# Seven-product down chunks from the first turn in three feed-forwards, from the fourth in the first

## The chip, the cores and the metric

The kernel runs on one core of one Trainium2 chip. The metric is the device time of one execution in microseconds, as the median of several runs. A profile is one execution recorded by the hardware profiler; its span is the time from the first to the last instruction. The engines are TensorE (PE in the rows; PEld is its weight load), VectorE (DVE), ScalarE (ACT), GpSimd (POOL) and the DMA queue of SyncE (SP).

## What is computed

Two decoder layers over 256 tokens of 1024 features, all in fp32. Each layer has a feed-forward, a mixer, a cross-attention to a memory of 256 tokens, and a second feed-forward. There are thus four feed-forwards, f = 0 to 3, and each computes

```python
h = rmsnorm(x, norm_w[layer, i])                      # i = 0 or 3
x = x + 0.5 * ((silu(h @ w_gate) * (h @ w_up)) @ w_down)   # 1024 -> 2816 -> 1024
```

The memory is normed once (`memn = rmsnorm(mem, mem_norm_w)`) and used by both cross-attentions. The rest of the layers is untouched by the change.

## The kernel before

Each fp32 product is made of three passes: both factors are split into a high part (rounded to the fp32r format by ScalarE) and a low part (the rest, by VectorE's subtraction), and TensorE adds high x high, high x low and low x high in PSUM. A split of a weight chunk of 128 x 2048 is one ScalarE copy and one VectorE subtraction.

Weights stream from HBM through a ring of three slots (`raw`, `w_hi`, `w_lo`), one megabyte each. A feed-forward has 11 hidden blocks of 256 features, j = 0 to 10 (`FJ` = 11). Its chunks come in the order gate 0, up 0, gate 1, up 1, down 0, gate 2, up 2, down 1 and so on, 33 in all, counted from `base`: down 0 is chunk `base + 4`. In its turn j TensorE multiplies gate j and up j (16 matmuls of 512 columns and 16 of 256 each) and then down j-1. VectorE and ScalarE in their turn j handle block j: they bring gate and up out of PSUM (banks 0 and 1, banks 2 and 3), scale, take the silu, multiply (`gu`), split the hidden block, and split the chunks that come next. Each engine runs its own list of instructions in the written order and meets the others at semaphores. A turn's order is written out by hand; nothing is planned at run time.

A plain down chunk is a block product with 2 x 2 x 2 = 8 products of 128 x 128 by 128 x 512, that is 24 matmuls (`down`, PSUM banks 4 to 7, which accumulate over all j). A seven-product chunk ("mixed") is one step of a Strassen-Winograd scheme, 7 products or 21 matmuls (`mixed_down`). It needs sums of blocks beforehand: three of the hidden block (`gu_sum`, line 1562), and four of the weights (`w_sum`, line 1556), of which one is written in place into the raw slot; then splits of the seven forms (`forms`, `forms_low`) and of the three weight sums (`Mixed.w_hi`, `Mixed.w_lo`). Products 3, 4 and 5 of the seven accumulate in banks 5, 4 and 7; products 1, 2, 6 and 7 go alone to banks 0, 1, 2 and 3, which TensorE may write only when gate and up of the next block have been read, and ScalarE copies these out (`copied`). The copies are added up in SBUF, in `Mixed.kept`, by accumulating DMAs that POOL issues.

Which chunks are mixed is in `Mixed.TURN` (first mixed j) and `Mixed.COUNT` (how many), one value for each feed-forward:

```python
TURN, COUNT = (4, 1, 1, 1), (5, 8, 8, 8)
```

So down 4 to 8 are mixed in f = 0 and down 1 to 8 in the others; the rest are plain. What TensorE waits for before a mixed chunk stands in its `turn`:

```python
pe.wait_ge(lo_done, j * 3 + (n + 3 - 3))
...
pe.wait_ge(gate_read, j + (f * FJ + 1))
pe.wait_ge(gu_done, j + f * FJ)
used(mixed_down(n + 2, f, j, mixed))
```

The count `lo_done` is brought to that value by VectorE's last step of the mixed turn, `Mixed.w_lo` (line 1618), and `gate_read` by the gate sum (line 1520) of the following turn. Within the chunk TensorE waits for `up_read` (line 1531) before it writes bank 2. SP loads down j+1 into the slot of down j when the latter is split: `lo_done` for a plain chunk, `down_split` for a mixed one.

In f = 0, turn 3 of ScalarE and VectorE also makes the high and low parts of the transposed memory (`mem_hi`, `mem_lo`), and turn 4 of ScalarE takes the squares of the memory's rows. The transposed memory lies in `xn`, where `Mixed.kept` lies too.

Of the kernel before, what the change touches and what calls it, by code (L numbers as in the profile page):

```python
# [20 lines left out]
F32 = mybir.dt.float32  # L21
F32R = mybir.dt.float32r
BF16 = mybir.dt.bfloat16
ALU = mybir.AluOpType
# [6 lines left out]
KT = D // P  # L31
# [5 lines left out]
RING = 3  # L37
# [127 lines left out]
def build(nc, d, out):  # L165
# [3 lines left out]
    with ctx:  # L169
# [277 lines left out]
        class Mixed:  # L447
            TURN, COUNT = (4, 1, 1, 1), (5, 8, 8, 8)
# [201 lines left out]
        def _(sp):  # L650
# [13 lines left out]
            def ffn(layer, which, first=False):  # L664
# [51 lines left out]
                else:  # L716
                    turn(0)
                    turn(1)
# [23 lines left out]
        def _(act):  # L742
# [115 lines left out]
            def ffn(layer, which):  # L858
# [91 lines left out]
                else:  # L950
# [5 lines left out]
                    silu(0)  # L956
                    hi_upto(base + 5)
                    hidden(f * FJ + 1, gu_hi)
                if f == 0:

                    turn(1)
                    turn(2)
                    turn(3, lambda c: mem_hi(range(3 * c, min(3 * c + 3, KT))))
                    turn(4, lambda c: c and squares(1, mem_rows, lambda t, h: act.wait_ge(mem_in, 16), tiles=(c - 1,)),
                         mixed=0)
                else:
                    turn(1, mixed=0)
                first = Mixed.TURN[f]
                turn(first + 1, mixed=1, out=0)
# [389 lines left out]
        def _(dve):  # L1359
# [154 lines left out]
            def ffn(layer, which):  # L1514
# [48 lines left out]

                def mixed_out(i, half, count):
# [23 lines left out]
                def turn_mixed(j, i):  # L1588
# [12 lines left out]
                    gu_sum(i, 0, gu_forms[:, 0:3:2, :], gu_forms[:, 2:5:2, :], gu_forms[:, 1:3, :], ALU.subtract)  # L1601
                    gu_sum(i, 1, gu_forms[:, 5, :], gu_forms[:, 2, :], gu_forms[:, 1, :], ALU.add)
                    gu_sum(i, 2, gu_forms[:, 6, :], gu_forms[:, 3, :], gu_forms[:, 5, :], ALU.subtract)
# [62 lines left out]
                else:  # L1666
                    lo_upto(base + 3)
                    gate_sum(0)
                    lo_upto(base + 4)
                    up_sum(0)  # L1670
                dve.wait_ge(row_read, row_no(norm_no(layer, 3 * which)))
# [7 lines left out]
                else:  # L1679
                    product(0)  # L1680
                    lo_upto(base + 5)
                    hidden_lo(0, gu_hi, gu_lo)
                if f == 0:
                    turn(1)
                    turn(2)
                    turn(3, lambda c: mem_lo(range(3 * c, min(3 * c + 3, KT))))
                first = Mixed.TURN[f]
                turn_mixed(first, 0)
# [587 lines left out]
        def _(pe):  # L2276
# [55 lines left out]
            def down(n, a_hi, a_lo, first, final, last_bank=None, between=lambda i: None, order=BLOCKS,  # L2332
                     second_half=None):

                for i, (t, h) in enumerate(order):
# [12 lines left out]
                    for k in range(2):  # L2348
                        if second_half and i == 0 and k:
# [4 lines left out]
                                        first and k == 0, final and k == 1)  # L2354
# [5 lines left out]
            def mixed_down(n, f, j, i):  # L2360
# [763 lines left out]
```

## Time and profile before

| | |
|---|---|
| Median of 3 runs | 1174.61 us (1174.28 to 1174.80) |
| Profiled execution | 1174.84 us |
| Span of the profiled execution | 1172.7 us |
| TensorE busy | 1165.1 us, 99% |
| VectorE busy | 979.0 us, 83% |
| ScalarE busy | 747.1 us, 64% |
| Mixed down chunks | 29 of 44 |

In the rows a timeline line gives start and duration in microseconds, the engine, the line of the kernel, the operation, output and input tiles, shapes, how many instructions were merged, and in brackets how long the engine had been idle and what ended that. Weight load and matmul overlap, and a matmul's listed duration overlaps the next one's: the spacing of starts is the time that counts.

### The profile page before, as it was taken

The numbers are of one execution on the slowest core, as the hardware profiler recorded it, in microseconds if no ns is written. First come the engines' busy times: TensorE is split into PE (matmuls) and PEld (weight loads), VectorE is DVE, ScalarE is ACT, GpSimd is POOL, SyncE is SP. The second block draws the span as 40 slices with busy tenths as digits, with TensorE's granted clock in tenths as the row PEclk, the third lists the DMA queues.
The fourth block names the chain that finished last, engine by engine and source line by source line (L and its number), as shares of the span: only waits on it lengthen the run. The fifth ranks groups of instructions, "written<-read, shape, count | busy, mean of one in ns | idle before, by whom it ended". The sixth has DMA issues, their size and how long they took to land.

```text
span 1172.7 us, 17754 instructions
## 1 busy us (share of the span) xinstructions
PE 1165.1 (99%) x6754; PEld 1019.4 (87%) x6754; DVE 979.0 (83%) x1134; ACT 747.1 (64%) x960; POOL 141.5 (12%) x139
## 2 busy tenths in 40 slices
PE   9999999999999999999999999999999999999998
PEld 8888889889989888888888888889887898888886
DVE  6689997875657589999988999997886676899997
ACT  7567766854457566777565777564576566677773
POOL 1000021520142010110010011010012121101000
PEclk9999999999999999999999999999999999999999
DMA  9957985454445455899755799846623334669991
GB/s 316 338 193 215 247 255 179 145 181 143 144 144 180 144 181 184 252 264 274 226 196 179 218 261 262 263 144 214 210 90 133 134 119 158 231 206 266 273 260 57
DMA packets 170056, 236.88 MB, mean 202 GB/s; under 512 B 15504, under 2 KB 139792, under 8 KB 169872
## 3 DMA queue, kind: packets, MB, share of 16 engines
q1 hardware_dynamic: 163664, 213.30, 55.5%
q0 software_dynamic: 6192, 22.55, 9.6%
q8 instruction: 38, 0.62, 0.2%
q10 hardware_dynamic: 144, 0.26, 0.1%
q14 instruction: 18, 0.15, 0.0%
HBM read 213.02 MB, written 1.05 MB: 183 GB/s over the span
## 4 chain that ended last, share of the span: by engine, by line
PE 99%; DMA 0%; DVE 0%; POOL 0%; issue 0%; POOLq 0%; ACT 0%; DVEq 0%; SPq 0%; ACTq 0%
PE ps L2302 30%; PE ps L2309 16%; PE ps L2281 15%; PE ps L2282 14%; PE ps L2283 14%; PE ps L2384 1%; PE ps L2569 1%; PE ps L3033 1%; PE ps L2889 1%; PE ps L3056 0%; PE ps L2577 0%; DMA arena<-in_first 0%; PE ps L2994 0%; PE ps L2991 0%; PE ps L2452 0%; PE ps L2641 0%
## 5 line engine op out<-in xcount | busy, mean ns | idle before, releaser
L2302 PE MATMUL ps<-hT,w_parts 128*128 128x512 f32 x1568 | 374.9, 391 | 0.9 <-DVE hT L1416 0.9
L2302 PEld LDWEIGHTS ps<-hT,w_parts 128*128 128x128 f32 x1568 | 290.1, 188 | 59.1 <-DVE w_parts L1443 0.7
L1374 DVE TENSOR_TENSOR w_parts<-raw,w_parts 128x2048 fp32r<-128x2048 f32 x85 | 195.9, 2314 | 57.9 <-ACT w_parts L758 57.8
L758 ACT ACTIVATE w_parts<-raw 128x2048 fp32r<-128x2048 f32 x85 | 162.3, 1920 | 73.5 <-PE ps L2283 71.0
L2309 PEld LDWEIGHTS ps<-hT,w_parts 128*128 128x128 f32 x1568 | 201.4, 191 | 8.0 <-DVE w_parts L1450 0.2
L2309 PE MATMUL ps<-hT,w_parts 128*128 128x256 f32 x1568 | 204.1, 283 | 0.0
L898 ACT ACTIVATE w_parts<-raw 128x2048 fp32r<-128x2048 f32 x79 | 150.9, 1910 | 1.0 <-DMA raw<-in_ffn_w_gate 1.0
L1592 DVE TENSOR_TENSOR w_parts<-raw,w_parts 128x2048 fp32r<-128x2048 f32 x58 | 132.5, 2284 | 0.4 <-ACT w_parts L898 0.4
L2236 POOL DMA_DIRECT2D xn<-arena x42 | 36.5, 868 | 503.7 <-ACT arena L909 503.7
L2281 PE MATMUL ps<-w_parts,hT 128*128 128x512 f32 (+1 forms) x240 | 91.0, 379 | 0.0
L2283 PE MATMUL ps<-w_parts,hT 128*128 128x512 f32 (+1 forms) x240 | 90.1, 375 | 0.0
L2282 PE MATMUL ps<-w_parts,hT 128*128 128x512 f32 (+1 forms) x240 | 90.1, 375 | 0.0
L2281 PE MATMUL ps<-w_parts,arena_r 128*128 128x512 f32 x204 | 79.9, 392 | 0.0
L2282 PE MATMUL ps<-w_parts,arena_r 128*128 128x512 f32 x204 | 79.8, 391 | 0.0
L2283 PE MATMUL ps<-w_parts,arena_r 128*128 128x512 f32 x204 | 79.4, 389 | 0.0
L1615 DVE TENSOR_TENSOR w_parts<-raw,w_parts 128x2048 fp32r<-128x2048 f32 x29 | 66.3, 2285 | 0.0
L880 ACT ACTIVATE arena<-ps 128x512 f32<-128x512 f32 x44 | 26.3, 597 | 62.7 <-PE ps L2309 62.6
L929 ACT ACTIVATE w_parts<-raw 128x2048 fp32r<-128x2048 f32 x29 | 55.3, 1906 | 0.0
L931 ACT ACTIVATE mixed_parts<-arena 128x1536 fp32r<-128x1536 f32 x29 | 43.2, 1491 | 18.3 <-DVE arena L1556 18.3
L909 ACT ACTIVATE arena<-ps 128x1024 f32<-128x1024 f32 x42 | 42.8, 1019 | 18.2 <-PE ps L2283 18.2
L873 ACT ACTIVATE arena<-arena 128x512 f32<-128x512 f32 x44 | 27.8, 631 | 40.6 <-DVE arena L1525 40.4
L2281 PEld LDWEIGHTS ps<-w_parts,hT 128*128 128x128 f32 x240 | 45.2, 188 | 8.5 <-DVE hT L1483 0.4
(365 smaller groups left out, 2176.4 us busy)
## 6 DMA issues: line engine op xcount, KB each, us to landing
raw<-in_ffn_w_down SPq DMA_DIRECT2D x44, 1024.0 KB, 6.8
raw<-in_ffn_w_gate SPq DMA_DIRECT2D x43, 1024.0 KB, 5.2
raw<-in_ffn_w_up SPq DMA_DIRECT2D x43, 1024.0 KB, 6.4
xn<-arena POOLq DMA_DIRECT2D x42, 512.0 KB, 6.9
raw<-in_xattn_wkv SPq DMA_DIRECT2D x16, 1024.0 KB, 5.4
raw<-in_even_w_in SPq DMA_DIRECT2D x13, 1024.0 KB, 5.0
raw<-in_xattn_wq SPq DMA_DIRECT2D x8, 1024.0 KB, 5.1
raw<-in_xattn_wo SPq DMA_DIRECT2D x8, 1024.0 KB, 4.9
```

What stands on the lines that cost most here:

```text
L758: ins = nc.scalar.activation(hi, src, ACT.Copy)
L898: nc.scalar.activation(w_hi[:, m % RING, :], raw[:, m % RING, :], ACT.Copy).then_inc(hi_done, 1)
L929: nc.scalar.activation(w_hi[:, m, :], raw[:, m, :], ACT.Copy).then_inc(hi_done, 1)
L931: nc.scalar.activation(Mixed.w_hi, Mixed.w_sums, ACT.Copy).then_inc(w_sums_hi, 1)
L1374: ins = V.tensor_tensor(lo, src, hi.bitcast(F32), ALU.subtract)
L1592: V.tensor_tensor(w_lo[:, m % RING, :], raw[:, m % RING, :], w_hi[:, m % RING, :].bitcast(F32), ALU.subtract).then_inc(lo_done, 1)
L1615: V.tensor_tensor(w_lo[:, m, :], raw[:, m, :], w_hi[:, m, :].bitcast(F32), ALU.subtract).then_inc(down_split, 1)
L2281: mm(dst, l_hi, r_hi, start=start, stop=False)
L2282: mm(dst, l_hi, r_lo, start=False, stop=False)
L2283: return mm(dst, l_lo, r_hi, start=False, stop=stop)
L2302: mm(ps[:, bank0 + m, :], cols(w_hi, n, k, CW, m * P, (m + 1) * P), hT[:, k, :, :].rearrange("p a c -> p (a c)"), start=k == 0, stop=False)
L2309: last = mm(ps[:, bank0 + m, SEQ:], cols(w_lo, n, k, CW, m * P, (m + 1) * P), hT[:, k, 0, :], start=False, stop=k == KT - 1)
```

## The change

The change lets the mixed chunks begin with down 0 in f = 1, 2 and 3, and with down 3 in f = 0. That makes 33 mixed chunks of 44. The work for down 0 is put into turn 0 of VectorE and ScalarE, which is written out apart from the loop. In VectorE's turn 0 the wait for the landed down chunk and the first two weight sums come between the gate sum and the split of up 1; the other two come behind the up sum. Bank 6 is not written by mixed chunks, so its first writer in the later feed-forwards is the plain chunk 9, which gets the flag `fresh`. The memory's parts move from turn 3 to turn 2, the squares from turn 4 to turn 3, and ScalarE waits for the memory's parts before the first copy to `Mixed.kept`.

```diff
-            TURN, COUNT = (4, 1, 1, 1), (5, 8, 8, 8)
+            TURN, COUNT = (3, 0, 0, 0), (6, 9, 9, 9)
...
                     turn(0)
-                    turn(1)
+                    turn(1, True)
...
                     silu(0)
+                    act.wait_ge(w_summed, w_sums_at(f, 0) + 2)
                     hi_upto(base + 5)
-                    hidden(f * FJ + 1, gu_hi)
+                    forms(0)
+                    act.wait_ge(w_summed, w_sums_at(f, 0) + 4)
+                    nc.scalar.activation(Mixed.w_hi, Mixed.w_sums, ACT.Copy).then_inc(w_sums_hi, 1)
                 if f == 0:
 
                     turn(1)
-                    turn(2)
-                    turn(3, lambda c: mem_hi(range(3 * c, min(3 * c + 3, KT))))
-                    turn(4, lambda c: c and squares(1, mem_rows, lambda t, h: act.wait_ge(mem_in, 16), tiles=(c - 1,)),
+                    turn(2, lambda c: mem_hi(range(3 * c, min(3 * c + 3, KT))))
+                    turn(3, lambda c: c and squares(1, mem_rows, lambda t, h: act.wait_ge(mem_in, 16), tiles=(c - 1,)),
                          mixed=0)
-                else:
-                    turn(1, mixed=0)
                 first = Mixed.TURN[f]
+                if f == 0:
+                    act.wait_ge(turned_done, 2 * KT)
...
+                def gu_sums(i):
+
+                    gu_sum(i, 0, gu_forms[:, 0:3:2, :], gu_forms[:, 2:5:2, :], gu_forms[:, 1:3, :], ALU.subtract)
+                    gu_sum(i, 1, gu_forms[:, 5, :], gu_forms[:, 2, :], gu_forms[:, 1, :], ALU.add)
+                    gu_sum(i, 2, gu_forms[:, 6, :], gu_forms[:, 3, :], gu_forms[:, 5, :], ALU.subtract)
...
                 else:
+                    n, m = base + 4, (base + 4) % RING
                     lo_upto(base + 3)
                     gate_sum(0)
+                    dve.wait_ge(raw_in[m], landed(n))
+                    w_sum(0, 0, Mixed.w_sums[:, 0, :], slot[:, 2, :], slot[:, 0, :], ALU.add)
+                    dve.wait_ge(w_summed, w_sums_at(f, 0) + 1)
+                    w_sum(0, 1, slot[:, 0, :], slot[:, 1, :], slot[:, 0, :], ALU.subtract)
                     lo_upto(base + 4)
                     up_sum(0)
+                    w_sum(0, 2, Mixed.w_sums[:, 1, :], slot[:, 2, :], slot[:, 0, :], ALU.subtract)
+                    w_sum(0, 3, Mixed.w_sums[:, 2, :], slot[:, 3, :], Mixed.w_sums[:, 1, :], ALU.subtract)
                 dve.wait_ge(row_read, row_no(norm_no(layer, 3 * which)))
                 gate_scale(0)
...
                     product(0)
-                    lo_upto(base + 5)
-                    hidden_lo(0, gu_hi, gu_lo)
+                    dve.wait_ge(mult_done, f * FJ + 1)
+                    gu_sums(0)
+                    dve.wait_ge(hi_done, n + 1)
+                    V.tensor_tensor(w_lo[:, m, :], raw[:, m, :], w_hi[:, m, :].bitcast(F32),
+                                    ALU.subtract).then_inc(down_split, 1)
+                    forms_low(0)
+                    dve.wait_ge(w_sums_hi, w_sums_hi_at(f, 0) + 1)
+                    V.tensor_tensor(Mixed.w_lo, Mixed.w_sums, Mixed.w_hi.bitcast(F32), ALU.subtract).then_inc(lo_done, 1)
...
                         last = product3(ps[:, 4 + 2 * t + h, :], a_hi[:, k, ts], a_lo[:, k, ts],
                                         cols(w_hi, n, k, D, h * 512, (h + 1) * 512),
                                         cols(w_lo, n, k, D, h * 512, (h + 1) * 512),
-                                        first and k == 0, final and k == 1)
+                                        (first or (t, h) in fresh) and k == 0, final and k == 1)
...
-            def mixed_down(n, f, j, i):
+            def mixed_down(n, f, j, fresh):
...
-                                    alone, alone)
+                                    alone or fresh, alone)
...
                 first = Mixed.TURN[f] + 1
                 if f == 0:
+                    turn(1, True)
                     with pe.Fori(2, first) as j:
                         turn(j, False)
-                turn(first, False, mixed=0)
+                    turn(first, False, mixed=0)
+                else:
+                    turn(1, True, mixed=0)
                 with pe.Fori(1, Mixed.COUNT[f]) as i:
                     turn(i + first, False, kept=i, mixed=i)
-                turn(FJ - 1, False, held=f == 3, kept=Mixed.COUNT[f])
+                turn(FJ - 1, False, held=f == 3, kept=Mixed.COUNT[f], fresh=((1, 0),) if f else ())
```

## Rows read from the trace of the kernel before

**Rows 1.** Page, part 1: busy time (share of the span) and instructions of each engine.

```profile
PE 1165.1 (99%) x6754; PEld 1019.4 (87%) x6754; DVE 979.0 (83%) x1134; ACT 747.1 (64%) x960; POOL 141.5 (12%) x139
```

**Rows 2.** Waits of TensorE's matmuls, whole span: who, for whom, us, times, longest.

```profile
PE ps L2302 <- DVE hT L1416: 0.9, 2, 0.5
PE ps L3069 <- POOL neg_half L2239: 0.9, 1, 0.9
```

**Rows 3.** Spans and clocks: span and mean granted TensorE clock of the core.

```profile
core 0: 1172.7 us, clock 1.000
```

**Rows 4.** Timeline of TensorE: first matmul of a down chunk, f=1, 2, 3.

```profile
438.68 0.40 PE L2281 MATMUL ps<-w_parts,arena_r 128*128 128x512 f32 x1
...
455.25 0.40 PE L2281 MATMUL ps<-w_parts,arena_r 128*128 128x512 f32 x1
...
471.15 0.40 PE L2281 MATMUL ps<-w_parts,arena_r 128*128 128x512 f32 x1
...
623.38 0.40 PE L2281 MATMUL ps<-w_parts,arena_r 128*128 128x512 f32 x1
...
1012.10 0.40 PE L2281 MATMUL ps<-w_parts,arena_r 128*128 128x512 f32 x1
```

**Rows 5.** Timelines of VectorE and TensorE, f=0, around the second mixed chunk.

```profile
92.63 0.68 DVE L1520 TENSOR_TENSOR arena<-arena,ps 128x512 f32<-128x512 f32 x1
...
96.26 0.40 PE L2281 MATMUL ps<-w_parts,arena_r 128*128 128x512 f32 x1
```

**Rows 6.** Transposed memory: its issue, its landing (KB, us), ScalarE in turn 2.

```profile
30.56 0.67 SPq L703 DMA_DIRECT2D xn<-in_memT  x1
...
xn<-in_memT SPq DMA_DIRECT2D x1, 1024.0 KB, 8.6
...
46.74 0.60 ACT L880 ACTIVATE arena<-ps 128x512 f32<-128x512 f32 x1 [2.15 <-PE ps L2309]
```

**Rows 7.** Timeline of VectorE in a steady mixed turn, f=3.

```profile
1121.19 0.68 DVE L1520 TENSOR_TENSOR arena<-arena,ps 128x512 f32<-128x512 f32 x1
...
1127.47 0.69 DVE L1556 TENSOR_TENSOR arena<-raw 128x512 f32<-128x512 f32 x1
1128.20 0.69 DVE L1556 TENSOR_TENSOR raw<-raw 128x512 f32<-128x512 f32 x1
1128.81 2.28 DVE L1592 TENSOR_TENSOR w_parts<-raw,w_parts 128x2048 fp32r<-128x2048 f32 x1
...
1131.61 1.09 DVE L1543 TENSOR_TENSOR arena_r<-arena,arena_r 128x896 fp32r<-128x896 f32 x1
...
1135.42 1.75 DVE L1618 TENSOR_TENSOR mixed_parts<-arena,mixed_parts 128x1536 fp32r<-128x1536 f32 x1
1137.09 0.68 DVE L1520 TENSOR_TENSOR arena<-arena,ps 128x512 f32<-128x512 f32 x1
```

**Rows 8.** Timelines of VectorE and ScalarE, f=2, turn 0, around the silu.

```profile
613.22 0.68 DVE L1525 TENSOR_TENSOR arena<-arena 128x512 f32<-128x512 f32 x1
...
613.93 0.63 ACT L873 ACTIVATE arena<-arena 128x512 f32<-128x512 f32 x1 [1.08 <-DVE arena L1525]
614.47 1.90 ACT L758 ACTIVATE w_parts<-raw 128x2048 fp32r<-128x2048 f32 x1
```

**Rows 9.** Down chunk 0 of f=1, 2, 3: issue (start), and landing (KB, us).

```profile
419.12 0.37 SPq L689 DMA_DIRECT2D raw<-in_ffn_w_down  x1
raw<-in_ffn_w_down SPq DMA_DIRECT2D x1, 1024.0 KB, 5.8
...
603.80 0.37 SPq L689 DMA_DIRECT2D raw<-in_ffn_w_down  x1
raw<-in_ffn_w_down SPq DMA_DIRECT2D x1, 1024.0 KB, 5.5
...
994.21 0.37 SPq L689 DMA_DIRECT2D raw<-in_ffn_w_down  x1
raw<-in_ffn_w_down SPq DMA_DIRECT2D x1, 1024.0 KB, 4.7
```

More of the change, by code:

```diff
@@ L1600, in turn_mixed @@
                     dve.wait_ge(mult_done, j + (f * FJ + 1))
-                    gu_sum(i, 0, gu_forms[:, 0:3:2, :], gu_forms[:, 2:5:2, :], gu_forms[:, 1:3, :], ALU.subtract)
-                    gu_sum(i, 1, gu_forms[:, 5, :], gu_forms[:, 2, :], gu_forms[:, 1, :], ALU.add)
-                    gu_sum(i, 2, gu_forms[:, 6, :], gu_forms[:, 3, :], gu_forms[:, 5, :], ALU.subtract)
+                    gu_sums(i)
                     n, m = base + 4 + RING, (base + 4) % RING
@@ L1680, in ffn @@
                     product(0)
-                    lo_upto(base + 5)
-                    hidden_lo(0, gu_hi, gu_lo)
+                    dve.wait_ge(mult_done, f * FJ + 1)
[6 more added lines that the diff above has]
+                    V.tensor_tensor(Mixed.w_lo, Mixed.w_sums, Mixed.w_hi.bitcast(F32), ALU.subtract).then_inc(lo_done, 1)
+                first = Mixed.TURN[f]
                 if f == 0:
                     turn(1)
[L1685 to L1688, printed above, removed]
+                    turn(2, lambda c: mem_lo(range(3 * c, min(3 * c + 3, KT))))
+                    turn_mixed(first, 0)
                 with dve.Fori(1, Mixed.COUNT[f]) as i:
@@ L2332, in down @@
             def down(n, a_hi, a_lo, first, final, last_bank=None, between=lambda i: None, order=BLOCKS,
-                     second_half=None):
+                     second_half=None, fresh=()):
                 for i, (t, h) in enumerate(order):
@@ L2464, in ffn, with hidden_down @@
                 f, base = 2 * layer + which, at["ffn", layer, which]
-                def hidden_down(j, n, first, final, between=lambda i: None, second_half=None):
+                def hidden_down(j, n, first, final, between=lambda i: None, second_half=None, fresh=()):
                     pe.wait_ge(gu_done, j)
                     used(down(n, gu_hi_last if final else gu_hi, gu_lo_last if final else gu_lo, first, final,
-                              between=between, second_half=second_half))
+                              between=between, second_half=second_half, fresh=fresh))
                 v = norm_no(layer, 3 * which)
@@ L2506, in ffn, with turn @@
                     rstd_rows(v, 5)
-                def turn(j, first, held=False, kept=None, mixed=None):
+                def turn(j, first, held=False, kept=None, mixed=None, fresh=()):
                     n = base + 2
@@ L2534, in turn @@
                         pe.wait_ge(gu_done, j + f * FJ)
-                        used(mixed_down(n + 2, f, j, mixed))
+                        used(mixed_down(n + 2, f, j, first))
                         pe.wait_ge(mixed_read, mixed * 2 + (mixed_read_at(f, 0) + 1))
@@ L2539, in turn @@
                         pe.wait_ge(gu_done, j + f * FJ)
-                        down(n + 2, gu_hi, gu_lo, False, False, order=BLOCKS[:3])
+                        down(n + 2, gu_hi, gu_lo, False, False, order=BLOCKS[:3], fresh=fresh)
                         return
-                    hidden_down(j + f * FJ, n + 2, first, False)
-                turn(1, True)
+                    hidden_down(j + f * FJ, n + 2, first, False, fresh=fresh)
                 first = Mixed.TURN[f] + 1
                 if f == 0:
+                    turn(1, True)
                     with pe.Fori(2, first) as j:
                         turn(j, False)
-                turn(first, False, mixed=0)
+                    turn(first, False, mixed=0)
+                else:
+                    turn(1, True, mixed=0)
                 with pe.Fori(1, Mixed.COUNT[f]) as i:
                     turn(i + first, False, kept=i, mixed=i)
-                turn(FJ - 1, False, held=f == 3, kept=Mixed.COUNT[f])
+                turn(FJ - 1, False, held=f == 3, kept=Mixed.COUNT[f], fresh=((1, 0),) if f else ())
                 n = base + FFN_CHUNKS - 1
```

## The prediction

> **What bounds the kernel.** I read the page's busy line first. TensorE is busy in 99% of the span, VectorE in 83%, ScalarE in 64% [rows 1]. The list of waits then says whether anybody holds TensorE up: its matmuls waited 0.9 us for VectorE and 0.9 for POOL, both in the opening of the program, and no other wait is listed [rows 2]. The granted clock is full throughout [rows 3]. So time follows the number of matmuls, as long as nothing starts to hold TensorE up. Fewer matmuls are a sure gain; the question is whether the work that pays for them, on VectorE and ScalarE, is ready in time. I therefore went to TensorE's timeline for the moments at which down chunks start, and then to VectorE's and ScalarE's timelines for the same stretch.
>
> **What is removed.** In the second feed-forward (f=1) the plain down chunk 0 starts at 438.68, the seven-product chunk 1 at 455.25 and chunk 2 at 471.15 [rows 4]. From start to start a turn with an eight-product (24 matmuls) down chunk takes 16.57 us, one with a seven-product (21 matmuls) 15.90 us. The difference is 0.67 us, three matmuls at 0.223 us. Four chunks change kind: down chunk 3 of the first feed-forward, down chunk 0 of the three later ones. That is 4 x 0.67 = 2.7 us off TensorE. In the other direction, the `fresh` flag only moves a `start` bit, and costs nothing.
>
> **First feed-forward (f=0).** The mixed sequence starts one turn earlier, in the middle of a run of alike turns. Today, when the second mixed chunk is due on TensorE at 96.26, the last thing it needs, VectorE's gate sum of the following chunk, started at 92.63 and takes 0.68: it is 2.9 us early [rows 5]. The first mixed chunk moves into the same pattern 16.6 us earlier, so the lead should stay at 2 to 3 us, and the 0.67 us is kept. Memory's parts move to the turn before. Their source is issued at 30.56 and lands 8.6 us later, at 39.2; ScalarE would read it after the silu of turn 2, and stood idle for 2.15 us before 46.74 in that turn [rows 6]. Three parts take 1.3 us there. Nothing on TensorE waits for them before the first norm. Cost 0; if the cover failed, the parts' 1.3 us beyond the idle time could show once. The new wait of ScalarE for `turned_done` stands behind work long finished: 0. SP's move (down chunk 4, or 1, waits for `down_split`) delays an issue by a few microseconds of which the load has spare ones: the steady turns run in that very order.
>
> **The later three: does VectorE finish in time?** Here TensorE may start down chunk 0 only when VectorE has finished the low parts of the three weight sums (`Mixed.w_lo`) and then the gate sum of chunk 1, because the mixed product writes banks 0 and 1. None of these was asked of it before. VectorE takes its instructions in order, and the new order puts the first weight sum, which waits for the landing of down chunk 0, ahead of the split of up chunk 1. The spacings come from a steady turn [rows 7] and from the silu of f=2 [rows 8]: a dependent pair of 512-column operations starts 0.73 us apart (1127.47 to 1128.20), an independent one 0.61 (1128.20 to 1128.81), a 2048-column low split takes 2.80 - 0.61 = 2.19 until the next starts (1128.81 to 1131.61). Other operations hand over about 0.08 before their listed end. From the first weight sum at 0:
>
> - second weight sum 0.73; low split of up chunk 1 at 1.34; up sum at 3.53; third weight sum 4.14; fourth (dependent) 4.87; gate scale 5.48
> - ScalarE's silu starts 0.71 after the gate scale (613.22 to 613.93): 6.19. The high part of down chunk 0 follows 0.54 after (613.93 to 614.47): 6.73, and takes 1.90: 8.63
> - VectorE meanwhile does the product (6.85) and the form sums (7.58, done 8.6); low split of down chunk 0 from 8.67; low forms 10.86 (1.09 - 0.08); `Mixed.w_lo` 11.86 (1.75 - 0.08); gate sum of chunk 1 at 13.53, done at 14.21.
>
> The landings are 5.8, 5.5 and 4.7 us behind issues at 419.12, 603.80 and 994.21 [rows 9], thus 424.9, 609.3 and 998.9. Adding 14.21: the gate sum is done at 439.13, 623.51, 1013.12. TensorE would be there at 438.68, 623.38, 1012.10 [rows 4]. So it waits 0.45 + 0.13 + 1.02 = 1.6 us. Nothing hides this, as TensorE has no other work ready. Handing over by semaphore is not in these numbers: ScalarE starts 0.03 us behind VectorE's end in rows 8, while the wait of TensorE in the opening is not finely resolved. For the two hand-overs (DMA to VectorE, VectorE to TensorE) I take 0.2 us a feed-forward, 0.6 in all; the bounds are 0.1 and 1.2 (a whole weight load, 0.19 each, exposed twice).
>
> **A second wait inside the chunk.** The sixth product writes bank 2 and waits for the up sum of chunk 1. Behind the gate sum come gate scale, the low split of gate chunk 2, and then that up sum: done 0.73 + 0.61 + 2.19 + 0.69 = 4.22 after the gate sum's start, 3.54 after its end. TensorE gets there after 15 matmuls at the 0.223 us found above, 3.35 us after its start. With the hand-over it waits some 0.2 us, three times: 0.6. Bounds: 0 and 1.0.
>
> **After the first chunk.** VectorE's mixed turn lasts 15.90 (1121.19 to 1137.09 [rows 7]), and in it VectorE twice waits a little at its up sum, for ScalarE; adding up the hand-overs listed above without that gives some 15.75 (an estimate) against TensorE's 15.90. The next gate sum then ends about 0.4 us before TensorE wants it, and the lead grows by 0.15 a turn. I take further waits as 0. What VectorE had before, two to three and a half microseconds of lead, is gone for the rest of the feed-forward.
>
> The extra pair of accumulating transfers per feed-forward (one more `i` in the POOL loop, two of 512 KB) lies beside work: the same pairs run in the turns of today. 0.
>
> **Sum**, against the profiled execution of 1174.84 us (span 1172.7 and 2.1 around it): -2.7 + 1.6 + 0.6 + 0.6 = +0.1. The profiled execution is 0.23 above the median of 1174.61, so the median should come to 1174.7. Bounds for this case: with a chain 0.3 us shorter in each of the three (0.9 us of waiting left), 0.1 of hand-over and nothing at bank 2 the sum is -1.7, 1172.9; with a chain 0.5 longer (3.1), 1.2 and 1.0 it is +2.6, 1177.2.
>
> One rule speaks against any change that makes TensorE wait. Rows 3 show a mean granted clock of 1.000, the 2.4 GHz level, although TensorE waited in the opening [rows 2]. The Trainium skill (TensorE: Matmul & The Clock Gate, Part 1) says that idleness drops the array to half clock, at which a matmul of 512 columns is spaced by 427 ns; by an estimate from that figure, a fallen clock would cost 0.2 us for every matmul until it rose again. The trace shows no fall, and waits of a microsecond are close to the one it shows without one. I give that 0.02.
>
> **Rivals.**
>
> 1. *The waits are absorbed; the full 2.7 us arrives.* It needs a chain 0.6 to 1.2 us shorter than mine: the landing earlier, or VectorE's order less tight. For it: in f=1 VectorE is free a microsecond before the landing, and the f=2 shortfall is only 0.13. Against it: in f=3 even an immediate landing leaves TensorE at the limit. Time 1174.6 - 2.7 = 1171.9.
> 2. *Slower: VectorE becomes the bound through the whole of a later feed-forward.* Place: turns 1 to 8 of f=1, 2, 3. With no lead left and 15.75 against 15.90, any 0.2 us more per turn on VectorE (a down chunk landing late beside the accumulating transfers, the up sum reaching bank 2 late) goes straight to TensorE. For it: the lead is 0.4 us where it was over 2. Against it: the turn of rows 7 already includes those transfers. It decides from a VectorE turn above 15.90. At 0.2 us in each of 24 turns: +4.8, 1179.3.
> 3. *It does not do what it says*: were the added chunks to run 24 matmuls after all, only the waits would stay. The loop counts (6, 9, 9, 9) exclude it; under 0.01.
>
> **Numbers.** Likeliest case 0.66 (1174.7, own range 1172.9 to 1177.2), rival 1 0.15, rival 2 0.17, clock 0.02. A measurement of this kernel tells a change from none at about 0.2%, that is 2.35 us: 1172.26 and 1176.96. Faster: rival 1 and a tail of the first case, 0.18. Slower: rival 2 and the clock, less the milder forms of rival 2, and a tail: 0.17. Same: 0.65. Range 1171.8 to 1177.6, which takes in rival 1 and the mild half of rival 2.
>
> **What would show it.** 12 fewer matmuls in the down chunks; 0 new waits of TensorE in f=0. In f=1, 2 and 3 one idle spot ahead of down chunk 0, released by VectorE's gate sum (line 1520), of 0.65, 0.35 and 1.2 us, and a smaller one at its bank 2, released by the up sum. Then turns at 15.90. The forecast is wrong if TensorE's waits add up to under 0.4 us (faster) or over 5 us (slower), or if the idle spots are released by another instruction.

## The result and the profile after

| | before | after |
|---|---|---|
| median of 11 runs each, us | 1174.61 | 1176.14 |
| lowest to highest, us | 1174.28 to 1174.93 | 1175.29 to 1180.43 |
| profiled execution, span, us | 1174.84, 1172.7 | 1176.10, 1174.3 |
| matmuls, TensorE busy us | 6754, 1165.1 | 6742, 1164.5 |

The ratio is 1.002 (95% interval 1.0012 to 1.0028); the two medians alone give 1.0013. By the bound that the prediction set, +1.53 us or 0.13% is no change; the forecast of +0.1 was 1.4 us too low; the interval leaves out a change of zero, and reaches past 0.2%. The second line is the less expected one: the runs of before lie within 0.7 us, those of after within 5.1. Outside the span, between the time of the profiled execution and its span, lie 2.1 us before and 1.8 in after and in every other changed kernel; no run shows why.

The page of after, part 1, and the clock of the core:

```profile
PE 1164.5 (99%) x6742; PEld 1018.1 (87%) x6742; DVE 997.6 (85%) x1166; ACT 759.0 (65%) x972; POOL 146.8 (13%) x147
```

```profile
core 0: 1174.3 us, clock 0.998
```

Against [rows 1] there are 12 matmuls fewer and 32 instructions of VectorE more, 18.6 us of its time. The clock, 1.000 in [rows 3], is at 1.00 in all three first turns and on to 1165; what is missing lies behind that, where the last matmuls and the output are (0.77 from 1165 to 1175, and 0.83 before).

TensorE's waits, whole span (who, for whom, us, times, longest), to be held against [rows 2]:

```profile
PE ps L2299 <- DVE mixed_parts L1701: 1.2, 1, 1.2
PE ps L2299 <- DVE arena L1522: 1.0, 1, 1.0
PE ps L3089 <- POOL neg_half L2257: 0.9, 1, 0.9
```

The first two are new, and stand where the prediction had put them. In f=3 the profile names the step ahead of the gate sum, `Mixed.w_lo`, as the releaser; by the times it was the gate sum, for TensorE starts 0.70 us behind the listed end of `Mixed.w_lo` (1011.95) and 0.10 behind that of the gate sum (1012.55). TensorE's timeline of after, first matmul of down chunk 0 in f=1, 2, 3 (start, us), answers to [rows 4]:

```profile
438.79 0.47 PE L2299 MATMUL ps<-w_parts,arena_r 128*128 128x512 f32 x1 [1.02 <-DVE arena L1522]
...
623.17 0.47 PE L2299 MATMUL ps<-w_parts,arena_r 128*128 128x512 f32 x1
...
1012.65 0.47 PE L2299 MATMUL ps<-w_parts,arena_r 128*128 128x512 f32 x1 [1.20 <-DVE mixed_parts L1701]
...
1016.16 0.47 PE L2299 MATMUL ps<-mixed_parts,arena_r 128*128 128x512 f32 x1
```

A matmul that follows a pause lasts 0.47 and not 0.40: at 623.17 and at 1016.16 (bank 2) there was a pause too short for the profile to name. VectorE's timeline of f=1 after shows the chain that was worked out:

```profile
424.33 0.69 DVE L1558 TENSOR_TENSOR arena<-raw 128x512 f32<-128x512 f32 x1 [1.58 <-DMA raw<-in_ffn_w_down]
...
425.66 2.28 DVE L1376 TENSOR_TENSOR w_parts<-raw,w_parts 128x2048 fp32r<-128x2048 f32 x1
...
429.79 0.68 DVE L1527 TENSOR_TENSOR arena<-arena 128x512 f32<-128x512 f32 x1
431.17 0.69 DVE L1541 TENSOR_TENSOR arena<-arena 128x512 f32<-128x512 f32 x1 [0.70 <-ACT arena L873]
...
436.19 1.75 DVE L1701 TENSOR_TENSOR mixed_parts<-arena,mixed_parts 128x1536 fp32r<-128x1536 f32 x1
437.86 0.68 DVE L1522 TENSOR_TENSOR arena<-arena,ps 128x512 f32<-128x512 f32 x1
```

From the first weight sum (424.33) to the end of the gate sum (438.54) it is 14.21 us, the forecast to the hundredth. Two idle spots stand in these rows: 1.58 us ahead of the chain, for the landing, and 0.70 inside it, for ScalarE's silu.

**Where the time went.** The start of the same instruction in both traces, a chunk or so ahead of down chunk 0 and the first behind it, then the last matmul. Before:

```profile
415.96 3.82 PE L2302 MATMUL ps<-hT,w_parts 128*128 128x512 f32 x16
...
444.15 2.20 PE L2302 MATMUL ps<-hT,w_parts 128*128 128x512 f32 x9
...
617.81 3.82 PE L2302 MATMUL ps<-hT,w_parts 128*128 128x512 f32 x16
...
628.84 1.52 PE L2302 MATMUL ps<-hT,w_parts 128*128 128x512 f32 x6
...
1000.86 3.92 PE L2302 MATMUL ps<-hT,w_parts 128*128 128x512 f32 x16
...
1017.56 3.79 PE L2302 MATMUL ps<-hT,w_parts 128*128 128x512 f32 x16
...
1166.67 0.28 PE L2283 MATMUL ps<-w_parts,mixed_parts 128*128 128x256 f32 x1
```

After:

```profile
414.88 3.36 PE L2320 MATMUL ps<-hT,w_parts 128*128 128x512 f32 x14
...
443.65 2.66 PE L2320 MATMUL ps<-hT,w_parts 128*128 128x512 f32 x11
...
617.31 2.00 PE L2320 MATMUL ps<-hT,w_parts 128*128 128x512 f32 x8
...
628.09 2.21 PE L2320 MATMUL ps<-hT,w_parts 128*128 128x512 f32 x9
...
1000.06 3.24 PE L2320 MATMUL ps<-hT,w_parts 128*128 128x512 f32 x13
...
1017.62 3.81 PE L2320 MATMUL ps<-hT,w_parts 128*128 128x512 f32 x16
...
1167.59 0.28 PE L2301 MATMUL ps<-w_parts,mixed_parts 128*128 128x256 f32 x1
```

After stands at -1.08 before f=1 (0.37 of it from the opening, 0.68 from f=0's three matmuls), at -0.50 behind its down chunk 0, at -0.75 behind that of f=2, at +0.06 behind that of f=3, and at +0.92 at the last matmul; what follows the last matmul adds 0.7. So the first turns cost net +0.58, -0.25 and +0.86. With the 0.67 that each saved, TensorE lost 1.25, 0.42 and 1.53 us in them, 3.2 in all. Two further losses came on top: 0.86 in the rest of f=3, and 0.7 at the end.

*The rest of f=3.* Call VectorE's lead the time from the end of its gate sum to TensorE's start of the down chunk. Before it is 2.15 us in the steady turns. In after it is 0.50, 0.58 and 0.12 at down chunk 1 of f=1, 2, 3 and grows by some 0.16 a turn in f=1 and f=2, but from down chunk 2 of f=3 (0.35) by 0.07 to 0.08, to 0.80 at down chunk 8. There VectorE's up sum starts 2.05 us behind the chunk's start (1140.17) for 0.83 before (1139.92), and the sum that takes the last products out of PSUM (line 1580, before 1572) ends at 1144.81. TensorE's next gate chunk starts 0.37 us later, 0.22 late. Timelines of VectorE and TensorE, after:

```profile
1142.22 0.68 DVE L1533 TENSOR_TENSOR arena<-arena,ps 128x512 f32<-128x512 f32 x1
...
1143.60 1.21 DVE L1580 TENSOR_TENSOR xn<-xn,ps 128x1024 f32<-128x1024 f32 x1
...
1145.18 3.91 PE L2320 MATMUL ps<-hT,w_parts 128*128 128x512 f32 x16
```

Before:

```profile
1140.75 0.69 DVE L1531 TENSOR_TENSOR arena<-arena,ps 128x512 f32<-128x512 f32 x1
...
1144.71 3.79 PE L2302 MATMUL ps<-hT,w_parts 128*128 128x512 f32 x16
```

Such pauses, too short for the list of waits, make up the 0.86: about 0.2 behind down chunk 0, 0.2 here, the rest from there to the last down chunk.

*The end.* From the last matmul to the end of the span it is 6.0 us before, 6.2 in the kernels below that change one feed-forward, 6.5 in those that change three and 6.7 in all that change four: 0.16 for each added mixed chunk. The prediction had the added pair of accumulating transfers at 0; that they are what adds this is not shown.

### The profile page after: what moved, and what is told of

Its sections match the earlier page's. It is cut to its first block, busy times and chain, and to the rows that moved or that the text cites. A ratio compares the mean times of both kernels' runs of the same rounds, so it can differ in the third digit from the quotient of the medians.

```text
span 1174.3 us, 17919 instructions
## 1 busy us (share of the span) xinstructions
PE 1164.5 (99%) x6742; PEld 1018.1 (87%) x6742; DVE 997.6 (85%) x1166; ACT 759.0 (65%) x972; POOL 146.8 (13%) x147
## 4 chain that ended last, share of the span: by engine, by line
PE 95%; DVE 3%; DMA 1%; issue 1%; ACT 0%; POOL 0%; POOLq 0%; DVEq 0%; ACTq 0%
PE ps L2320 28%; PE ps L2327 15%; PE ps L2299 15%; PE ps L2300 14%; PE ps L2301 14%; PE ps L2402 1%; DMA raw<-in_ffn_w_down 1%; DVE w_parts L1376 1%; PE ps L3053 1%; PE ps L2909 1%; PE ps L2589 1%; PE ps L3089 0%; PE ps L3076 0%; DVE hT L1408 0%; PE ps L3014 0%
## 5 line engine op out<-in xcount | busy, mean ns | idle before, releaser
L2254 POOL DMA_DIRECT2D xn<-arena x50 | 43.4, 868 | 498.8 <-ACT arena L909 498.8
L2299 PE MATMUL ps<-w_parts,arena_r 128*128 128x512 f32 x188 | 73.9, 393 | 2.4 <-DVE mixed_parts L1701 1.2
L2300 PE MATMUL ps<-w_parts,arena_r 128*128 128x512 f32 x188 | 73.6, 391 | 0.0
L2301 PE MATMUL ps<-w_parts,arena_r 128*128 128x512 f32 x188 | 73.2, 389 | 0.0
L909 ACT ACTIVATE arena<-ps 128x1024 f32<-128x1024 f32 x50 | 51.0, 1019 | 15.0 <-PE ps L2301 14.9
L1624 DVE TENSOR_TENSOR mixed_parts<-arena,mixed_parts 128x1536 fp32r<-128x1536 f32 x30 | 52.5, 1750 | 0.0
```

The source lines that it names most:

```text
L1624: V.tensor_tensor(Mixed.w_lo, Mixed.w_sums, Mixed.w_hi.bitcast(F32), ALU.subtract).then_inc(lo_done, 1)
L2299: mm(dst, l_hi, r_hi, start=start, stop=False)
L2300: mm(dst, l_hi, r_lo, start=False, stop=False)
L2301: return mm(dst, l_lo, r_hi, start=False, stop=stop)
```

## Experiments

All are timed against the kernel before on the same chip, which gave 1174.69 to 1174.83; each has its median and range. Three questions stood behind them: which part costs, which reason VectorE has to be late, and where the spread comes from.

**The parts.** `f0_only` keeps the first feed-forward's part: `TURN, COUNT = (3, 1, 1, 1), (6, 8, 8, 8)`.

> The change in the first feed-forward alone (down 3 mixed, memory's parts a turn earlier); the later three as before. Theory (each mixed chunk is 3 matmuls, 0.67 us, and nothing waits here): 1174.6 - 0.7 = 1173.9, spread of the runs as small as before (0.7 us), no new wait of TensorE. Rival (moving memory's parts costs time or makes the time unsteady): 1174.6 or more.

1174.39 (1173.69 to 1177.93), ratio 1.0 (0.9991 to 1.0009). The gain is 0.3 and not 0.7, and the spread is there with this part alone: a miss. Its trace has a wait of 0.46 us at 164.59, at the end of f=0, and 0.2 us of the loss stand at the end of the span.

`later_only` keeps the three others: `TURN, COUNT = (4, 0, 0, 0), (5, 9, 9, 9)`.

> The change in the later three alone, the first feed-forward as before. Theory (VectorE's chain in turn 0, started by the landing of down chunk 0, makes TensorE wait more than the 2.0 us that three chunks save): waits of 1.2, 0.4 and 1.5 us ahead of and inside down chunk 0 of f=1, 2, 3, some 0.9 us more at the end of f=3; about 1176.8, and the wide spread of the changed kernel (5 us) stays. Rival (the spread and the loss come from the first feed-forward): near 1172.6 and steady.

1176.75 (1175.81 to 1179.13), ratio 1.002 (1.001 to 1.0029): the time expected, but not by the parts expected. The 0.9 at the end of f=3 did not come. TensorE's waits were 1.12, 0.64 and 1.09 us, behind landings for which VectorE stood idle 1.67, 1.23 and 1.14: in f=2 twice the wait of after's profile, because the same transfer took 5.9 us and not 5.4. The three first turns cost net 0.71, 0.24 and 0.75 us. Another 0.71 was lost in f=0, which is as before the change: ScalarE stood idle 3.02 us for a gate chunk (at 142.05), and TensorE stopped at 164.90. So late landings in f=0 come in some executions without f=0's part, too.

`f3_only` changes the last feed-forward alone: `(4, 1, 1, 0), (5, 8, 8, 9)`, with the first turn of before wherever the count is 8.

> The change in the last feed-forward alone, the other three as before. By the offsets of the two traces it lost 0.86 us in its first turn and 0.7 more at its end, where its last down chunk finds VectorE without a lead: 1176.1. By the prediction's terms (1.02 us of wait and 0.4 of hand-over and second wait against 0.68 of matmuls) it costs 0.7 in the first turn and nothing further on: 1175.3.

1175.56 (1175.01 to 1176.46), +0.83: nearer to the prediction's terms. TensorE waits 1.14 us at down chunk 0, has lost 0.77 net by the end of it (1018.33 against 1017.56) and 0.88 at the last matmul. The further 0.86 of after's profile is therefore not what a lost lead costs each time; in `later_only` that stretch took 149.12 us, before 149.11. In `later_only` the lead in f=3 grew from 0.45 at down chunk 1 by 0.17 a turn, to 1.61 at down chunk 8, where after has 0.80.

**Why VectorE is late.** `two_more` repeats the first weight sum twice ahead of itself in the first turn (1.46 us of VectorE's time; the values do not change):

```
                     dve.wait_ge(raw_in[m], landed(n))
+                    for _ in range(2):
+                        step(V.tensor_tensor(Mixed.w_sums[:, 0, :], slot[:, 2, :], slot[:, 0, :], ALU.add))
```

> The changed kernel with two more 512-column operations (results overwritten) ahead of the first weight sum in VectorE's turn 0 of f=1, 2, 3, 1.46 us in all. Theory (the chain sets TensorE's start one to one): TensorE's waits at down chunk 0 grow by 1.46 us in each of the three, 4.4 us in all, 1180.5. Rival (TensorE is held by the landing of the loads or by ScalarE, VectorE's order has room): under 1 us more.

1185.12 (1182.88 to 1185.83), +8.98 on after: twice the expected. The waits did what was forecast: 2.25, 2.40 and 2.62 us, 7.27 against some 2.5 (1.02, 1.20 and, at 623.17 for an expected 622.88, 0.29), so +4.8. The other half is in the timeline of TensorE behind the wait, here in f=3:

```profile
1021.06 0.77 PE L2301 MATMUL ps<-w_parts,arena_r 128*128 128x512 f32 x1 [2.62 <-DVE arena L1522]
1021.63 0.63 PE L2302 MATMUL ps<-w_parts,arena_r 128*128 128x512 f32 x1
1022.06 0.63 PE L2303 MATMUL ps<-w_parts,arena_r 128*128 128x512 f32 x1
...
1024.73 0.40 PE L2301 MATMUL ps<-w_parts,arena_r 128*128 128x512 f32 x1
1024.96 0.40 PE L2302 MATMUL ps<-w_parts,arena_r 128*128 128x512 f32 x1
```

and in its windows (the column before the last two is the granted clock):

```profile
1000.00:1018.00 18.00, 18.00 (x108) 16.00 (x107) 15.03 (x18) 10.74 (x11) 4.96 (x6) 1.00 0.62 205
1018.00:1024.00 6.00, 3.38 (x11) 2.63 (x11) 5.96 (x6) 3.16 (x4) 0.00 (x0) 0.75 0.54 176
1024.00:1034.00 10.00, 10.00 (x52) 8.52 (x52) 9.67 (x12) 8.25 (x7) 0.00 (x0) 0.98 0.58 189
```

Matmuls start 0.43 us apart where they start 0.23 apart otherwise: TensorE is at its lower level, 1.2 GHz, for 3.4 us behind the wait. The first eight matmuls take 3.44 us (1021.06 to 1024.50) for 8 x 0.227 = 1.82. That is 1.6 us here, and by the same count 1.7 in f=1 and 1.5 in f=2, 4.8 in all: with the waits 9.6, for 9.0 measured. The rest of f=3 lost nothing here, where after lost 0.86, and with that taken off it is 8.7. VectorE, with TensorE stopped for so long, has its lead back (2.17 at down chunk 8). The Trainium skill (TensorE: Matmul & The Clock Gate, Part 1) gives this: idleness drops the array to the half clock, with 427 ns from start to start for 512 columns. The trace agrees, at 0.43.

`one_more` repeats it once.

> The changed kernel with one more weight sum (0.73 us) ahead of the first one in the first turn of each later feed-forward; two of them raised TensorE's waits to 2.25, 2.40 and 2.62 us, and behind each the granted clock was down for some 3 us. With one, the waits should be 1.75, 1.0 and 1.9 us: +2.2 us, 1178.3, if the clock stays at 1.00 behind them. If the clock falls behind the two longer ones as well, each costs 1.5 us more: 1181.3. Rival: all that two more cost beyond their waits was the lead that VectorE lost, not the clock: then half of the 9.0 us, 1180.6, with the clock at 1.00.

1180.19 (1179.40 to 1184.35), +4.05. The trace shows waits of 1.42, 1.52 and 2.05 us; the rows are TensorE's in f=1 and in f=3:

```profile
439.15 0.47 PE L2300 MATMUL ps<-w_parts,arena_r 128*128 128x512 f32 x1 [1.42 <-DVE arena L1522]
439.46 0.40 PE L2301 MATMUL ps<-w_parts,arena_r 128*128 128x512 f32 x1
```

```profile
1015.31 0.66 PE L2300 MATMUL ps<-w_parts,arena_r 128*128 128x512 f32 x1 [2.05 <-DVE arena L1522]
1015.77 0.63 PE L2301 MATMUL ps<-w_parts,arena_r 128*128 128x512 f32 x1
```

Behind 1.42 and 1.52 the clock stayed, behind 2.05 it fell: nine matmuls take 3.72 us for 2.05, another 1.7. The profiled execution (1179.40) had one fall; runs at 1183.55 and 1184.35 are 4 to 5 us above it. My sum (1178.3 or 1181.3) lies on either side; the rival, a lost lead with the clock at 1.00, came close in its number (1180.6) but is refuted by these rows, and by the rest of f=3, which lost nothing. By parts, 2.5 of added waits and 1.7 for the clock, less after's 0.86, are the 3.3 that lie between the two profiled executions.

**Two moves in VectorE's order.** `order_split_first` moves the split of up chunk 1 into the idle spot ahead of the chain:

```
+                    lo_upto(base + 4)
                     dve.wait_ge(raw_in[m], landed(n))
                     w_sum(0, 0, ...)
                     dve.wait_ge(w_summed, w_sums_at(f, 0) + 1)
                     w_sum(0, 1, ...)
-                    lo_upto(base + 4)
```

> The changed kernel with one move alone: in the first turn of the three later feed-forwards VectorE splits up chunk 1 ahead of the first two weight sums instead of behind them. If the waits come from how late down chunk 0 lands plus the 14.2 us of VectorE's work behind it, the split (2.2 us) now fills the 1.58, 0.70 and 1.23 us in which VectorE stood idle for the landing, the gate sum of chunk 1 ends at about 437.0, 622.3 and 1011.3, and TensorE's waits of 1.02, 0.3 and 1.20 us go down to 0, 0 and 0.3: 1176.1 less 2.2 and less some of the 0.7 that f=3 loses at its end is 1173.6, and the spread of the runs shrinks. Rival: the chain from the weight sums over ScalarE's copy of them to their low part sets the wait, and moving the sums back by the split only makes that later: 1176 to 1178.

1174.09 (1173.47 to 1176.57), ratio 0.9997 (0.9988 to 1.0006). All listed waits ahead of down chunk 0 are gone. 2.05 us won of the 2.5 expected. The lead at down chunk 0 is still only 0.26, 0.26 and 0.10 us, and the rest of f=3 loses 0.86 as in after.

`order_sums_later` takes weight sums 3 and 4 from before the gate's scale to behind the product:

> The changed kernel with the other move alone: the last two weight sums of the first turn (1.4 us) go from before the gate's scale to behind the product. VectorE has the same instructions between the landing of down chunk 0 and the gate sum of chunk 1, so by the theory of VectorE's chain nothing is won: TensorE's waits stay 1.0, 0.3 and 1.2 us, 1176.1. Rival: ScalarE's part (the hidden values' silu and high halves, which start sooner by 1.4 us) sets the waits, then they shrink by up to 1.4 each and the time is 1173.5.

1174.98 (1174.19 to 1179.48), between the two. I had counted instructions and overlooked the idle 0.70 us for the silu inside the chain. The two sums now fill it: 13.34 us from the first weight sum (425.43) to the end of the gate sum, 0.87 shorter. The listed waits ahead of down chunk 0 are 0.6 in f=3 and none in f=1 and 2. The rest of f=3 lost 0.89 here, and f=0 had two waits of 0.6 (at 159.25 and 165.01).

`order_both` makes both moves.

> The changed kernel with another order in VectorE's turn 0: the low split of up chunk 1 goes ahead of the first two weight sums, the other two weight sums go behind the gate scale. Nothing is added or taken away. Theory: from the spacings the gate sum of chunk 1 is then done 0.9 us before TensorE needs it in each of f=1, 2, 3; no wait at down chunk 0, the full saving of 2.7 us, 1171.9, and a small spread since the landing no longer sets the start of the chain. Rival (VectorE without its lead of over 2 us is the bound in all later turns): waits come back in turns 1 to 8, 1174 or more.

1173.07 (1172.51 to 1174.60), ratio 0.9986 (0.9977 to 0.9995), 3.07 under after. The lead at down chunk 0 is now 0.95 us, and the rest of f=3 loses 0.22. VectorE in f=1:

```profile
424.76 2.29 DVE L1376 TENSOR_TENSOR w_parts<-raw,w_parts 128x2048 fp32r<-128x2048 f32 x1 [0.43 <-ACT w_parts L758]
426.97 0.69 DVE L1558 TENSOR_TENSOR arena<-raw 128x512 f32<-128x512 f32 x1
...
437.55 0.68 DVE L1522 TENSOR_TENSOR arena<-arena,ps 128x512 f32<-128x512 f32 x1
```

The chain is 11.26 us, 2.20 (the split) and 0.75 (the silu's wait) less, and TensorE starts down chunk 0 at 439.19 without a stop. One new wait is left in the whole span, at the end of f=0:

```profile
PE ps L2320 <- DVE xn L1580: 0.6, 1, 0.6
```

**The first feed-forward and the spread.** `order_later_only` is `order_both` with `TURN, COUNT = (4, 0, 0, 0), (5, 9, 9, 9)`.

> Both moves in the three later feed-forwards, and the first feed-forward as before the change (seven products from its fifth turn). Against both moves with all four parts changed (1173.07 us) this gives back the 12 products' share of one chunk, 0.67 us, and takes away the wait of 0.5 to 0.6 us at 165 us in the first feed-forward: 1173.2. If the first feed-forward's late transfers are the source of the spread, the runs lie within 1 us of each other; if the spread comes from the later feed-forwards, they lie over 2 us apart as before.

1172.52 (1172.35 to 1172.69), ratio 0.9981 (0.9972 to 0.9990). The runs lie within 0.34 us, and the time is 0.55 lower than with f=0's part, which should have saved 0.67: that part costs. In the trace of `order_both`, VectorE in f=0 waits for two down chunks that land late:

```profile
131.26 0.69 DVE L1558 TENSOR_TENSOR arena<-raw 128x512 f32<-128x512 f32 x1 [0.59 <-DMA raw<-in_ffn_w_down]
...
148.89 0.69 DVE L1558 TENSOR_TENSOR arena<-raw 128x512 f32<-128x512 f32 x1 [1.30 <-DMA raw<-in_ffn_w_down]
```

and SyncE's own timeline shows what surrounds the first of these transfers:

```profile
122.75 0.37 SPq L689 DMA_DIRECT2D raw<-in_ffn_w_down  x1
123.16 0.57 SPq L713 DMA_DIRECT2D conv_w<-in_ssm_conv_w  x1
123.78 6.99 SPq L713 DMA_DIRECT2D pe_pairs<-in_nsa_cmp_pe  x2
130.81 1.04 SPq L689 DMA_DIRECT2D raw<-in_ffn_w_gate  x1
```

The chunk issued at 122.75 needed 8.5 us; two small strided loads held the queue for 7.0 us right behind it, and the next gate chunk had to wait for them. Before the change they stood there too (6.0 us from 124.79), and the down chunk ahead of them came in time; the next one was late already then, by 0.44 us at 147.90 for 1.30 now. What differs is the load on the DMA engines: with accumulating transfers issued from 98.31 on (before from 115.09) their busy share from 106 to 115 is 0.97 for 0.82, and from there to 149 it is 0.99 to 1.10 (before 0.93 to 1.07, so the difference is small there), so a late transfer finds no gap to catch up in. That is a reading; the run that tests it is `strided_early`.

`strided_spread` spreads the strided loads over turns 6 to 9: `((6, (0, 3)), (7, (3, 5)), (8, (5, 6)), (9, (6, 7)))`.

> Both moves, all four feed-forwards changed, and SyncE's seven small strided loads, which stand behind turns 6 (four) and 7 (three) of the first feed-forward, spread over turns 6 to 9 (three, two, one, one). SyncE was held 5.7 and 7.0 us by them and issued the gate chunk behind the second group at 130.81. If they are what makes down chunks land late at 131 and 148 us (VectorE idle 0.6 and 1.3 us), those stops and TensorE's 0.6 us at 165 go: 1172.5, runs within 1 us. Rival: the accumulating transfers of the output, which now begin a turn sooner, take the bandwidth: 1173.1, the stops stay.

1177.20 (1175.55 to 1177.49), a clear miss. I had moved the last one past its reader. ScalarE stood behind it in f=0, and TensorE behind ScalarE; first ScalarE, then TensorE:

```profile
163.51 0.51 ACT L1306 ACTIVATE small_parts<-xk 128x64 fp32r<-128x64 f32 x2 [4.44 <-DMA pe_pairs<-in_nsa_cmp_pe]
```

```profile
165.28 0.80 PE L2297 MATMUL ps<-mixed_parts,arena_r 128*128 128x512 f32 x1 [3.03 <-DVE arena L1531]
165.87 0.63 PE L2298 MATMUL ps<-mixed_parts,arena_r 128*128 128x512 f32 x1
```

It shows the clock's fall once more, behind 3.03 us.

`strided_early` moves them the other way, to turns 2 to 5, with all else as `order_both`:

```
+                    early = dict(zip(range(2, 6), (strided_loads()[5:6], strided_loads()[6:7], strided_loads()[0:3], strided_loads()[3:5])))
+                    for j in range(2, 10):
                         turn(j, j > Mixed.TURN[f])
...
-                    for j, (a, b) in ((6, (0, 4)), (7, (4, 7))):
...
+                            for dst, src in early.get(j, ()):
```

> Both moves, all four feed-forwards changed, and the seven small strided loads moved forward to turns 2 to 5 of the first feed-forward (one, one, three, two), before its accumulating transfers begin, so that SyncE holds nothing in turns 6 and 7 and their consumer at 160 us has them in time. If they share the blame for the down chunks that land late at 131 and 148 us, TensorE's 0.6 us at 165 us go and the spread with them: 1172.0 (12 products less than both moves without the first feed-forward, 0.67 under 1172.5). Rival: the accumulating transfers alone are enough to make the loads late once they begin a turn sooner: 1173.1 with a spread of 2 us, as before the loads were moved.

1172.07 (1171.91 to 1172.57), ratio 0.9978 (0.9969 to 0.9986): the fastest of all, and steady. VectorE no longer waits for any down chunk in f=0. The rival is refuted: the accumulating transfers alone do not make them late. All seven strided loads moved at once, so the share of the four behind turn 6 and of the three behind turn 7 is not told apart. Its control, `early_later_only`, is the same with f=0 as before the change.

> The control for the earlier strided loads: both moves in the three later feed-forwards, the strided loads in turns 2 to 5, and the first feed-forward's seven products from its fifth turn as before the change. If the strided loads hurt only together with accumulating transfers that begin a turn sooner, this is 1172.5 as with the loads where they stood, and the 1172.07 with all four parts changed is the worth of the first feed-forward's part, 0.45 us of the 0.67 forecast. If moving the loads gains by itself, this is 1172.0 or less, and the first feed-forward's part is worth nothing even so.

1172.60 (1172.24 to 1172.74), ratio 0.998 (0.9971 to 0.9989). By itself the earlier loading gains nothing (1172.52 without it); with it, f=0's part is worth 0.53 us of the 0.67 forecast, and the 0.14 between them is about the 0.16 that each added mixed chunk costs at the end of the span. So that part loses through the loads that stand in its way, and beyond the end through nothing else of weight.

## Why the prediction was right, and where its steps were off

- *Likeliest case, 1174.7.* It came: neither the full 2.7 (rival 1), nor VectorE as the bound of all later turns (rival 2). The mechanism is the forecast one, and the chain's length, the matmuls and the place of the waits were right. The size was off by 1.2 us between the profiled executions (+1.26 for +0.1), made of 0.4 more in the first turns, 0.86 in the rest of f=3 and 0.65 at the end of the span, less 0.37 in the opening and 0.3 outside the span. The last two have nothing to do with any term; that they took 0.7 off the miss is luck.
- *Matmuls removed, 4 x 0.67.* Right: 12 fewer.
- *The chain, 14.21 us.* Right to the hundredth in f=1, and step by step (gate scale 5.46 for 5.48, `Mixed.w_lo` 11.86, gate sum 13.53); f=2 and f=3 end 14.21 behind theirs as well (608.70 to 622.91, 998.34 to 1012.55).
- *Waits of 0.45, 0.13 and 1.02, hand-overs 0.6, second wait 0.6: 2.8.* Measured 3.2 in the profiled execution (1.25, 0.42, 1.53), but the terms lie otherwise. The chunk's start came 1.2, 0.3 and 1.35 us late, 2.8 for the 2.2 of waits and hand-overs, and each first matmul cost 0.08 more. The second wait was 0.1 in f=3 and nothing in f=1 and f=2, for the forecast 0.6: an error the other way, which hid part of the first. The feed-forward that was off most is f=1: its landing took 6.2 us where [rows 9] had 5.8. The landing was read once and used as if fixed. In `later_only` f=2's took 5.9 for 5.5. Every tenth of a microsecond of landing goes straight through the chain into TensorE, which is why one profile could not fix this sum: the first turns of the three feed-forwards together cost net +1.7 in the profile of `later_only` where the terms give 3 x -0.67 + 2.8 = +0.8, and that of f=3 alone, with the steadiest landing (4.7 to 4.9), +0.77 in `f3_only` where they give +0.7.
- *First feed-forward: cost 0, no new wait.* This step failed, and so did the sentence on the accumulating transfers. The argument looked at one mixed chunk at 92.63 [rows 5]. What a chunk begun a turn sooner collides with is at 122 to 150 us: the strided loads. The part brought -0.3 (`f0_only`) or +0.55 (`order_both` against `order_later_only`) and not -0.67, and with the strided loads elsewhere -0.53. In after's own profiled execution it did bring the full saving inside f=0 (-0.68); there the landings happened to come in time for TensorE. The medians show that this is not the rule.
- *Further waits as 0.* Right in f=1 and f=2, where the lead was 0.50 and 0.58 at down chunk 1 (forecast about 0.4) and grew by some 0.16 a turn (forecast 0.15). This step failed in f=3: the lead began at 0.12 and then grew by 0.07 to 0.08 a turn, and the stretch lost 0.86. `order_split_first` and `order_sums_later` repeat it (0.86 and 0.89). The loss goes with the lead: none at 1.61 (`later_only`) or 2.17 (`two_more`), 0.1 at 1.33 (`f3_only`), 0.22 at 1.25 (`order_both`), 0.86 at 0.80, the leads all read at down chunk 8. It is a mild form of rival 2. The slow growth in f=3 is in the kernels that also change f=0 (after, `order_both` and `strided_early`, for instance) and not in `f3_only`, `later_only` and `order_later_only`; why is open.
- *Added accumulating transfers, 0.* The span's end is 0.16 us later for each added mixed chunk, 0.65 in after. Whether it is these transfers is open.
- *The clock, 0.02.* After's profiled execution has no fall: its waits are 1.02 and 1.20. But the argument "close to the one it shows without one" was about one execution. A wait of 2.05 us is enough, and costs 1.7 more. Landings that vary by half a microsecond bring after's waits towards that in some executions. That this is what makes runs of 1179 to 1180 is argued from `one_more` and from the spread vanishing together with the waits (0.34 and 0.66 us in `order_later_only` and `strided_early`); no execution of after at 1179 was profiled, so it is not shown. The mean granted clock of the single runs speaks rather against it: after's four slowest runs (1177.18 to 1180.43) have 0.998 and 0.999, as its others have, while `two_more` with three falls has 0.995 and the two slow runs of `one_more` 0.996. `order_split_first`, with no listed wait ahead of down chunk 0, still spreads over 3.1 us. One fall is about 0.0014 of the mean clock (half of 3.1 to 3.7 us in 1176), so the rounding leaves room for one in a run, hardly for more. Without any fall, f=0 alone went from -0.68 to +1.17 us between the profiled executions of after and `order_sums_later`, where its code is the same.

## What to carry to other kernels

Where an engine with its lead used up starts on a landing, read that landing in several traces, not one: its variation goes through to the bound engine, and here waits of 2.05 us and more also cost a fall of the clock. Follow the lead itself from turn to turn to the end of the loop, and compare what lies behind the last instruction of the bound engine: here 0.86 and 0.65 us lay in those two places. Then look at the order before giving the change up: work that needs nothing of the transfer belongs ahead of the wait for it, and work that nobody needs soon belongs into the wait inside the chain; two such moves turned +1.5 us into -1.5. And look at what small strided loads share the queue with when a transfer is moved to an earlier turn.

## What the runs showed of the hardware

- A pause of TensorE of 1.02 to 1.52 us left the granted clock at 1.00; 2.05, 2.25, 2.40, 2.62 and 3.03 us were each followed by a stretch at the lower level, with 512 columns 0.43 us apart for 0.23. The stretch lasted 3.7, 3.7, 3.1 and 3.4 us behind the first four of these pauses and cost 1.5 to 1.7 us (`one_more`, `two_more`; the last pause is of `strided_spread`).
- Two strided loads of 8 KB each held SyncE's queue for 7.0 us among chunk loads and accumulating transfers (3.03 us for one of them in `strided_early`, at 42.26), while the 1 MB chunk at 122.75 took 0.37 to issue.
- The same 1 MB chunk landed in 5.4 (after) and in 5.9 us (`later_only`), two kernels that are equal around it.
- The span ends 0.16 us later for each mixed chunk added: 6.0 us behind the last matmul with none, 6.2 with one, 6.5 with three, 6.7 with four.
